# Cutting VectorE's routing of two heads into a key part and a pair part, in six gaps instead of three

## The chip, the cores and the metric

The kernel runs on one core of a Trainium2 chip. The metric is the device time of one execution in microseconds (us), the median of several runs. In the profile PE is TensorE's matmuls, PEld its weight loads, DVE VectorE, ACT ScalarE, POOL GpSimd and SP SyncE.

## The reference, cut to what matters

Two decoder layers over 256 tokens of width 1024. Layer 0 mixes tokens by a gated linear recurrence, layer 1 by dilated attention, and each is followed by a PEER expert layer. That one is where most of the time goes:

```python
q = (xn @ w_q).reshape(T, PEER_HEADS, PEER_DKEY)          # 8 heads
s1 = einsum('thd,nd->thn', q[..., :half], sub_keys[0])    # 128 keys each
s2 = einsum('thd,nd->thn', q[..., half:], sub_keys[1])
v1, i1 = lax.top_k(s1, 16);  v2, i2 = lax.top_k(s2, 16)
cand = (v1[..., :, None] + v2[..., None, :]).reshape(T, 8, 256)
cs, ci = lax.top_k(cand, 16)
experts = i1[ci // 16] * 128 + i2[ci % 16];  gates = softmax(cs)
act = gelu(xn . u[experts]) * gates
out = sum over the 128 experts of act * v[experts]
```

Each token gathers 128 rows of 4 KB from `u` and 128 from `v`.

## The kernel before

Tokens lie on the 128 partitions, in two tiles. Layer and tile make four phases: (0,0), (0,1), (1,0), (1,1). A phase's gather has 16 rounds, and a round handles eight experts of each token, half a head. GpSimd copies the eight indices to `idx_cur` and issues eight indirect DMAs into `u_ring` and eight into `v_ring` (eight slots each). An issue into a slot of u waits until VectorE has used the row before (L748, one instruction a row), one of v until TensorE has (L1240). VectorE multiplies each u row by the token and sums it, ScalarE takes a tanh (`ez`), VectorE writes the eight weights `act_w` (L762), ScalarE makes eight diagonal matrices `diag`, and TensorE adds diag times v row to `acc`, two matmuls of 512 columns a row.

All that a token tile needs before its gather (mixer, projection of the queries, key scores, routing) is written as generators with `yield`s, one set for each of the four compute engines, and `run` places their steps in the gaps between the rounds of the phase before: after round n, in gap n, each engine runs what `PLANS[phase][n]` names. "m" is the next step of the next phase's mixer and routing, "R" the next piece of this phase's own routing. Every engine works strictly in the order in which its program is written. In each gap VectorE's work comes behind `act_w` of that round and ahead of the u rows of the next. TensorE's comes behind the round's `acc` matmuls. ScalarE's comes behind the `diag`s and ahead of `ez` of the next round.

`PARTS` cuts the eight heads into (0), (1), (2, 3), (4, 5) and (6, 7). Heads 0 and 1 are routed with the steps of the phase before. Parts 2 to 4 are the "R" pieces, each in one gap: `route_part` on VectorE, one exponential of the gates on ScalarE, nothing on TensorE. GpSimd waits on `idx_ready` for the indices of a head, and head h is needed from round 2h.

The weights of mixers and projections come in 1 MB chunks on SP's queue into four slots of `w_ring`. SP issues the next chunk when TensorE has used the one four before.

Names for later: `tv`, `ti`, `tif` are the top 16 of a head's two key lists, `cand` their 256 sums, `cs`, `ci` the best 16 of these, `hot` (in the tile `xn`) a one-hot table that turns positions into key numbers. `xn` also holds the normed tokens that TensorE transposes for a mixer, hence the wait on `transposed` in `route_part`.

Of the kernel before, what the change touches and what calls it, by code (L numbers as in the profile page):

```python
# [35 lines left out]
TOPK = 16  # L36
PART = 2
PARTS = ((0, 1), (1, 1), (2, 2), (4, 2), (6, 2))
# [31 lines left out]


PLANS = {
    0: ["R", "m", "Rm", "R"] + ["m"] * 10 + ["", ""],
    1: ["R", "m", "Rm", "R"] + ["m"] * 11 + [""],
    2: ["R", "m", "Rm", "R"] + ["m"] * 11 + [""],
    3: ["R", "R", "R", ""],
}


class Chain:  # L80
# [10 lines left out]
    def link(self, ins):  # L91
        self.tick(ins)
        self.engine.wait_ge(self.sem, self.base + self.n if self.step is None else self.step + (self.base + self.n))
# [27 lines left out]
def build(nc, x_d, wall_d, gains_d, lb_d, headg_d, rope_d, amask_d, lmask_d, ident_d, iota_d, skt_d,  # L121
          u_d, v_d, out_d):
    ctx = ExitStack()
    with ctx:
# [3 lines left out]
        def sem(name):  # L128
            return ctx.enter_context(nc.semaphore(name))
# [63 lines left out]
        hot = xn[:, :].rearrange("p (m n) -> p m n", n=TOPK)  # L193
# [45 lines left out]
        transposed = sem("transposed")  # L239
# [17 lines left out]
        PHASE_OF = [(0, 0), (0, 1), (1, 0), (1, 1)]  # L257
# [119 lines left out]
        def _(dve):  # L377
# [3 lines left out]
            link, tick = chain.link, chain.tick  # L381
            count = Count()
# [4 lines left out]
            def wait_next(sem, n=1):  # L387
                dve.wait_ge(sem, count.next(sem.name, n))
# [17 lines left out]
            def token_rsqrt(t):  # L406

                link(V.scalar_tensor_tensor(out=xn[:, :], in0=h[:, t, :], scalar=1.0, in1=h[:, t, :],
                                            op0=ALU.mult, op1=ALU.mult, accum_out=ms[:, 0:1]))
                rsqrt(1, D)  # L410
# [6 lines left out]
            def scale_gain(t, gain, dst, scale):  # L417
                link(V.scalar_tensor_tensor(out=dst, in0=h[:, t, :], scalar=scale, in1=gains[:, gain, :],
                                            op0=ALU.mult, op1=ALU.mult))
                count.transposes += 1  # L420
                count.normed = count.transposes
                dve.sem_inc(to_transpose, 1)
# [216 lines left out]
                add_residual(t, 1, 1)  # L639
                dve.sem_inc(mixed, 1)  # L640

            def route_part(phase, p):

                layer, t = PHASE_OF[phase]
                lo, heads = PARTS[p]
                if p in (0, 2):

                    wait_next(projected)

                dve.wait_ge(transposed, count.normed)  # L650
                hot_n = hot[:, 0:2 * heads * TOPK, :]
                pairs = [(n, a) for n in range(heads) for a in range(2)]

                def each(ops, of):
                    for op in ops:
                        for m in of:
                            (link if op is ops[-1] and m is of[-1] else tick)(op(m))


                sc = lambda m: s_all[:, lo + m[0], m[1], :]  # L660
                first = lambda a, m: a[:, m[0], m[1], 0:8]
                last = lambda a, m: a[:, m[0], m[1], 8:16]
# [6 lines left out]
                for n in range(heads):  # L669
                    tick(tt(cand[:, n, :].rearrange("p (a b) -> p a b", a=TOPK), over(tv[:, n, 0, :], TOPK),  # L670
                            tv[:, n, 1:2, :].to_broadcast([P, TOPK, TOPK]), ALU.add))
                link(V.tensor_copy(tif[:, 0:heads, :, :], ti[:, 0:heads, :, :]))
                each([lambda n: V.max(cs[:, n, 0:8], cand[:, n, :])], range(heads))
                each([lambda n: V.max_index(ci[:, n, 0:8], cs[:, n, 0:8], cand[:, n, :]),
                      lambda n: V.match_replace(cand[:, n, :], cs[:, n, 0:8], cand[:, n, :], LOWEST)], range(heads))
# [30 lines left out]
            def route(phase):  # L706
                layer, t = PHASE_OF[phase]

                if phase == TILES:
                    dve.wait_ge(gain_in, 16)  # L710
                scale_gain(t, (GAIN_F0, GAIN_F1)[layer], xp[:, t, :], 1.0)
                token_rsqrt(t)
                link(V.tensor_copy(xr[:, t:t + 1], rs[:, 0:1]))
                dve.sem_inc(factor_ready, 1)
                yield

                dve.wait_ge(transposed, count.normed)
                link(V.tensor_scalar(xp[:, t, :], xp[:, t, :], xr[:, t:t + 1], None, ALU.mult))
                count.chunks += 8
                count.banks += 8  # L720
                route_part(phase, 0)
                yield
                route_part(phase, 1)
                yield rest(phase)

            def rest(phase):

                for p in range(2, len(PARTS)):
                    route_part(phase, p)
                    yield  # L730

            def mixer(phase):
# [66 lines left out]
            link(V.memset(ones[:, :], 1.0))  # L799
            dve.wait_ge(consts_in, 16 * EARLY)  # L800
            run(gather, mixer, route)


        @block.scalar
        def _(act):
            A = nc.scalar
            chain = Chain(act, act_side)
            link, tick = chain.link, chain.tick
            count = Count()
# [4 lines left out]
            def give(out, in_, func, **more):  # L814

                wait_next(argument)
                link(A.activation(out, in_, func, **more))  # L817
                act.sem_inc(value, 1)  # L818
# [111 lines left out]
            def route_part(phase, p):  # L930
                lo, heads = PARTS[p]
                g = gate_all[:, phase * SLOTS + lo * TOPK:phase * SLOTS + (lo + heads) * TOPK]
                give(g, g, ACT.Exp)

            def rest(phase):
                for p in range(2, len(PARTS)):
                    route_part(phase, p)
                    yield

# [65 lines left out]
        def _(pe):  # L1005
            M = nc.tensor.matmul
            count = Count()
# [169 lines left out]
            def rest(phase):  # L1177
                for p in range(2, len(PARTS)):
                    yield

            def route(phase):
                layer, t = PHASE_OF[phase]
                transpose_new([xp[:, t, n * P:(n + 1) * P] for n in range(KT_D)])
                turn_of = {}

                def queries(c):
                    project(1, True)
                    turn_of[c] = count.banks

                def scores(c):  # L1190
                    out = take_turn()

                    pe.wait_ge(bank_read, turn_of[c])
                    for b in range(4):
                        ins = M(out[:, b * P:(b + 1) * P], qpT[:, 4 * c + b, :], skt[:, layer, b % 2, :], start=True,  # L1195
                                stop=True)
                    ins.then_inc(scored, 1)

                queries(0)
                if phase == 0:  # L1200
                    pe.wait_ge(later_in, 16 * LATER)
                scores(0)
                yield
                queries(1)
                if phase == 0:

                    pe.wait_ge(w_used, WRING + count.chunks)
                    pe.sem_inc(u_used, RING)
                queries(2)
                scores(1)  # L1210
                scores(2)
                yield
                queries(3)
                if phase == 0:

                    pe.wait_ge(w_used, WRING + count.chunks)
                    pe.sem_inc(v_used, RING)
                scores(3)
                count.next(projected.name, 2)
                yield rest(phase)  # L1220
# [103 lines left out]
```

## Time and profile before

| | us |
|---|---|
| median of 3 runs | 1776.9 |
| lowest and highest | 1772.48 and 1778.13 |
| profiled execution, span from first to last instruction | 1768.2 |
| median less that span | 8.7 |
| TensorE busy | 1434.2 |
| VectorE busy | 1116.1 |
| GpSimd busy | 1143.6 |
| ScalarE busy | 276.3 |

The times of the runs are whole executions; the span is that of one profiled execution. Busy times are sums over the span, and an engine can be the one that sets the pace in one stretch and wait in the next.

### The profile page before, as it was taken

To read this page: it belongs to the slowest core of one execution; us is meant where nothing else is said; L and a number is where in the kernel's file an instruction comes from. 1 tells how busy PE (TensorE), PEld (TensorE's weight loads), DVE (VectorE), ACT (ScalarE), POOL (GpSimd) and SP (SyncE) were. 2 spreads that over 40 slices of the span, in tenths; PEclk is the share of its full clock that TensorE was granted. 3 is DMA by queue.
4 is the path that set the end of the run, shared out by engine and by line. 5 is a ranking of instruction groups with operands and counts; after the bars stand their busy time and mean duration, and the time that the engine had idled before them with its cause. 6 is when DMAs were issued, how large, how long until landed. Compare 5 with 4: busy or idle time off the path is not lost.

```text
span 1768.2 us, 18597 instructions
## 1 busy us (share of the span) xinstructions
PE 1434.2 (81%) x5144; PEld 835.4 (47%) x5144; DVE 1116.1 (63%) x2843; ACT 276.3 (16%) x757; POOL 1143.6 (65%) x1094
## 2 busy tenths in 40 slices
PE   7968797999898596988899778889789766776776
PEld 6867454655664253544357334454346422332332
DVE  2648786777463868475566578665567499444454
ACT  1211111211111111121111110122111101111111
POOL 0004777677657777767776676667775767777775
PEclk9989898999999898989899889899999987988889
DMA  8855999999999999999999999999999989999998
GB/s 321 307 217 178 352 414 410 410 411 410 413 399 411 341 370 392 377 381 384 374 413 412 386 322 413 358 408 374 372 397 411 339 317 326 354 358 369 368 389 327
DMA packets 164520, 649.13 MB, mean 367 GB/s; under 512 B 18656, under 2 KB 18912, under 8 KB 151648
## 3 DMA queue, kind: packets, MB, share of 16 engines
q0 software_dynamic: 147456, 536.94, 79.6%
q1 hardware_dynamic: 16992, 111.27, 15.8%
q8 instruction: 40, 0.66, 0.1%
q14 instruction: 32, 0.26, 0.0%
HBM read 647.09 MB, written 1.05 MB: 367 GB/s over the span
## 4 chain that ended last, share of the span: by engine, by line
PE 57%; DVE 21%; DMA 7%; issue 6%; POOL 5%; ACT 4%; POOLq 0%; DVEq 0%; ACTq 0%; SPq 0%; PEldq 0%
PE acc L1240 35%; PE bank L1061 9%; DVE u_ring L748 9%; PE bank L1057 8%; DMA u_ring<-in_u,idx_cur 6%; POOL v_ring L370 3%; POOL u_ring L370 2%; DVE xn L385 1%; ACT diag L988 1%; DVE arena L385 1%; ACT xT L825 1%; PE bank L1195 1%; DVE ef L692 1%; DMA v_ring<-in_v,idx_cur 1%; ACT arena L840 1%
## 5 line engine op out<-in xcount | busy, mean ns | idle before, releaser
L1240 PE MATMUL acc<-v_ring,diag 128*128 128x512 f32 x2040 | 972.8, 638 | 267.5 <-ACT diag L988 266.0
L1240 PEld LDWEIGHTS acc<-v_ring,diag 128*128 128x128 f32 x2040 | 413.2, 205 | 805.5 <-issue 569.1
L748 DVE SCALAR_TENSOR_TENSOR u_ring<-u_ring,xp 128x1024 f32<-128x1024 f32 x512 | 613.0, 1225 | 260.0 <-DMA u_ring<-in_u,idx_cur 250.0
L370 POOL DMA_INDIRECT v_ring<-in_v,idx_cur x512 | 578.5, 1130 | 270.4 <-PE acc L1240 135.5
L370 POOL DMA_INDIRECT u_ring<-in_u,idx_cur x512 | 539.7, 1054 | 195.0 <-issue 132.0
L1061 PE MATMUL bank<-w_ring,xT 128*128 128x256 f32 x768 | 171.9, 384 | 7.3 <-ACTq L826 7.3
L1061 PEld LDWEIGHTS bank<-w_ring,xT 128*128 128x128 f32 x768 | 146.6, 192 | 30.5 <-ACTq L826 8.9
L988 ACT ACTIVATE diag<-ident,act_w 128x128 f32<-128x128 f32 x510 | 156.2, 388 | 17.7 <-DVE act_w L762 15.9
L1057 PE MATMUL bank<-xT,w_ring 128*128 128x128 f32 x1280 | 148.4, 279 | 6.2 <-ACTq L826 6.2
L1057 PEld LDWEIGHTS bank<-xT,w_ring 128*128 128x128 f32 x1280 | 147.4, 195 | 11.4 <-ACTq L826 7.6
L762 DVE SCALAR_TENSOR_TENSOR act_w<-ez,gz 128x8 f32<-128x8 f32 x64 | 10.9, 170 | 197.1 <-ACT ez L983 197.1
L361 POOL COPY idx_cur<-idx_all 128x8 uint32 x64 | 23.4, 365 | 145.2 <-DVE idx_all L696 144.9
L983 ACT ACTIVATE ez<-zi 128x8 f32<-128x8 f32 x64 | 13.3, 208 | 539.9 <-DVEq L759 535.7
L840 ACT ACTIVATE arena<-bank 128x512 f32<-128x512 f32 (+1 forms) x54 | 30.3, 580 | 372.6 <-PE bank L1057 222.1
L385 DVE TENSOR_TENSOR arena<-arena 128x512 f32<-128x512 f32 (+3 forms) x57 | 42.9, 782 | 7.6 <-ACTq L818 4.4
L825 ACT ACTIVATE xT<-tr 128x512 f32<-128x512 f32 x26 | 14.2, 595 | 181.6 <-PE tr L1019 181.1
L748 DVE DVE_READ_ACCUMULATOR u_ring<-u_ring,xp 128x1 f32 x512 | 41.7, 81 | 0.0
L825 ACT ACTIVATE arena<-tr 128x512 f32<-128x512 f32 (+2 forms) x24 | 11.6, 524 | 152.8 <-PE tr L1173 106.8
L777 DVE COPY h<-acc 128x512 f32<-128x512 f32 x3 | 2.1, 692 | 47.1 <-PEq L1261 47.1
L817 ACT ACTIVATE arena<-arena 128x1024 f32<-128x1024 f32 x18 | 19.0, 1057 | 38.7 <-DVEq L425 38.4
L817 ACT ACTIVATE gate_all<-gate_all 128x32 f32<-128x32 f32 (+1 forms) x20 | 4.5, 224 | 124.0 <-DVEq L425 123.8
L385 DVE TENSOR_TENSOR h<-h,bank 128x512 f32<-128x512 f32 x8 | 5.5, 686 | 27.8 <-PE bank L1061 25.0
(128 smaller groups left out, 794.6 us busy)
## 6 DMA issues: line engine op xcount, KB each, us to landing
w_ring<-in_wall SPq DMA_DIRECT2D x92, 1024.0 KB, 8.5
u_ring<-in_u,idx_cur POOLq DMA_INDIRECT x512, 7.2
v_ring<-in_v,idx_cur POOLq DMA_INDIRECT x512, 7.1
u_ring<-in_wall SPq DMA_DIRECT2D x4, 1024.0 KB, 9.7
v_ring<-in_wall SPq DMA_DIRECT2D x4, 1024.0 KB, 9.8
gains<-in_gains SPq DMA_DIRECT2D x5, 512.0 KB, 13.4
h<-in_x SPq DMA_DIRECT2D x2, 512.0 KB, 9.1
arena<-in_amask SPq DMA_DIRECT2D x1, 576.0 KB, 10.3
```

Source lines behind the costliest of these rows:

```text
L361: nc.gpsimd.tensor_copy(idx_cur[:, g * RING:(g + 1) * RING], idx_all[:, bass.ds(i * TOPK + g * RING, RING)]).then_inc(idx_set, 1)
L370: nc.gpsimd.indirect_dma_start(out=ring[:, r, :], out_offset=None, in_=table, in_offset=bass.IndirectOffsetOnAxis(ap=idx_cur[:, g * RING + ...
L385: return V.tensor_tensor(out, a, b, op)
L692: link(V.tensor_reduce(ef[:, 0:heads, :, :].rearrange("p n a k -> p (n a k)"), hot_n, AX.X, ALU.add))
L748: V.scalar_tensor_tensor(out=u_ring[:, r, :], in0=u_ring[:, r, :], scalar=1.0, in1=xp[:, t, :], op0=ALU.mult, op1=ALU.mult, accum_out=z[:, ...
L817: link(A.activation(out, in_, func, **more))
L825: (link if n == len(copies) - 1 else tick)(A.activation(dst, src, ACT.Copy))
L840: A.activation(dst, source[:, first:first + width], func, scale=scale))
L988: A.activation(diag[:, r, :], ident[:, :], ACT.Copy, scale=act_w[:, g * RING + r:g * RING + r + 1]).then_inc(diag_ready, 1)
L1057: ins = M(out[:, (2 * c + b) * P:(2 * c + b + 1) * P], w[:, k, b * P:(b + 1) * P], xT[:, k, :], start=k == 0, stop=k == KT_D - 1)
L1061: ins = M(out[:, c * 256:(c + 1) * 256], xT[:, k, :], w[:, k, :], start=k == 0, stop=k == KT_D - 1)
L1240: ins = M(acc[:, s], diag[:, r, :], v_ring[:, r, s], start=False, stop=hi == ROUNDS and n == hi - lo - 1 and r == count_of - 1)
```

## The change

`route_part` of VectorE is cut in two. `key_part` finds the top 16 of the two key lists of each head, forms the 256 sums and casts the key numbers. `pair_part` finds the best 16 sums, the gates and the expert numbers, and gives `idx_ready`. For heads 0 and 1 both still run one after the other. For parts 2 to 4 there is a `yield` between them, so that there are six "R" pieces, and the plans are written anew. ScalarE and TensorE get empty pieces to match, and ScalarE's exponential goes with `pair_part`.

```diff
 PLANS = {
-    0: ["R", "m", "Rm", "R"] + ["m"] * 10 + ["", ""],
-    1: ["R", "m", "Rm", "R"] + ["m"] * 11 + [""],
-    2: ["R", "m", "Rm", "R"] + ["m"] * 11 + [""],
-    3: ["R", "R", "R", ""],
+    0: ["R", "Rm", "R", "Rm", "R", "Rm"] + ["m"] * 9 + [""],
+    1: ["R", "Rm", "R", "Rm", "Rm", "Rm"] + ["m"] * 9 + [""],
+    2: ["R", "Rm", "R", "Rm", "Rm", "Rm"] + ["m"] * 9 + [""],
+    3: ["R", "R", "R", "R", "R", "R"],
 }
...
-            def route_part(phase, p):
...
+            def key_part(p):
+
                 lo, heads = PARTS[p]
                 if p in (0, 2):
 
                     wait_next(projected)
-
-                dve.wait_ge(transposed, count.normed)
-                hot_n = hot[:, 0:2 * heads * TOPK, :]
                 pairs = [(n, a) for n in range(heads) for a in range(2)]
...
                 link(V.tensor_copy(tif[:, 0:heads, :, :], ti[:, 0:heads, :, :]))
+
+            def pair_part(phase, p):
+
+                layer, t = PHASE_OF[phase]
+                lo, heads = PARTS[p]
+                dve.wait_ge(transposed, count.normed)
+                hot_n = hot[:, 0:2 * heads * TOPK, :]
                 each([lambda n: V.max(cs[:, n, 0:8], cand[:, n, :])], range(heads))
...
-                route_part(phase, 0)
-                yield
-                route_part(phase, 1)
+                key_part(0)
+                pair_part(phase, 0)
+                yield
+                key_part(1)
+                pair_part(phase, 1)
                 yield rest(phase)
 
             def rest(phase):
 
                 for p in range(2, len(PARTS)):
-                    route_part(phase, p)
+                    key_part(p)
+                    yield
+                    pair_part(phase, p)
                     yield
...
 (ScalarE)
             def rest(phase):
                 for p in range(2, len(PARTS)):
+                    yield
                     route_part(phase, p)
                     yield
...
 (TensorE)
             def rest(phase):
                 for p in range(2, len(PARTS)):
                     yield
+                    yield
```

## Rows read from the trace of the kernel before

**Rows 1.** The page: span, engines, transfer rate by 40 slices, all transfers, issue to landing.
```profile
span 1768.2 us, 18597 instructions
...
PE 1434.2 (81%) x5144; PEld 835.4 (47%) x5144; DVE 1116.1 (63%) x2843; ACT 276.3 (16%) x757; POOL 1143.6 (65%) x1094
...
GB/s 321 307 217 178 352 414 410 410 411 410 413 399 411 341 370 392 377 381 384 374 413 412 386 322 413 358 408 374 372 397 411 339 317 326 354 358 369 368 389 327
DMA packets 164520, 649.13 MB, mean 367 GB/s; under 512 B 18656, under 2 KB 18912, under 8 KB 151648
...
u_ring<-in_u,idx_cur POOLq DMA_INDIRECT x512, 7.2
```

**Rows 2.** Windows by phase: us, busy us (PE to POOL), PEclk, DMA share, GB/s.
```profile
167.90:590.10 422.20, 366.47 (x1436) 222.38 (x1436) 286.54 (x714) 71.78 (x187) 298.92 (x282) 0.93 1.01 402
590.10:1001.20 411.10, 341.32 (x1118) 189.08 (x1118) 265.58 (x705) 63.23 (x188) 287.85 (x273) 0.92 0.99 384
1001.20:1411.30 410.10, 340.02 (x1154) 191.52 (x1154) 269.01 (x704) 66.26 (x192) 290.18 (x272) 0.95 0.99 377
1411.30:1753.80 342.50, 240.91 (x483) 102.28 (x484) 204.56 (x505) 42.56 (x144) 249.97 (x249) 0.85 0.96 358
```

**Rows 3.** Windows: phases 1 and 2, rounds 0-6; phase 3 rounds 2-4 and ten later ones, between issues.
```profile
590.10:778.90 188.80, 152.51 (x456) 85.91 (x456) 139.61 (x402) 27.64 (x83) 128.42 (x116) 0.92 0.97 373
1001.20:1190.60 189.40, 153.00 (x456) 86.15 (x456) 139.82 (x401) 27.67 (x83) 131.14 (x117) 0.92 0.98 372
1433.90:1509.80 75.90, 52.06 (x103) 22.34 (x104) 64.24 (x200) 11.29 (x38) 53.88 (x51) 0.80 0.92 327
1509.80:1734.20 224.40, 157.68 (x318) 66.71 (x317) 107.91 (x210) 26.53 (x90) 167.86 (x171) 0.86 0.98 371
```

**Rows 4.** Timeline of TensorE, phase 1; brackets: idle before and its releaser.
```profile
616.86 16.38 PE L1240 MATMUL acc<-v_ring,diag 128*128 128x512 f32 x32 [10.41 <-ACT diag L988]
...
635.33 7.17 PE L1061 MATMUL bank<-w_ring,xT 128*128 128x256 f32 x32 [1.22 <-ACTq L826]
644.15 14.00 PE L1240 MATMUL acc<-v_ring,diag 128*128 128x512 f32 x32 [1.65 <-ACT diag L988]
657.99 13.98 PE L1061 MATMUL bank<-w_ring,xT 128*128 128x256 f32 x64
...
700.07 15.73 PE L1240 MATMUL acc<-v_ring,diag 128*128 128x512 f32 x32 [12.38 <-ACT diag L988]
...
726.75 14.00 PE L1240 MATMUL acc<-v_ring,diag 128*128 128x512 f32 x32 [1.68 <-ACT diag L988]
```

**Rows 5.** Timeline of VectorE, phase 1, gap 0 and the start of gap 1.
```profile
590.02 0.87 DVE L663 MAX8 tv<-arena 128x8 f32<-128x128 f32 x4
...
596.17 0.75 DVE L673 MAX8 cs<-cand 128x8 f32<-128x256 f32 x2
...
605.93 1.22 DVE L748 SCALAR_TENSOR_TENSOR u_ring<-u_ring,xp 128x1024 f32<-128x1024 f32 x1
...
616.20 0.17 DVE L762 SCALAR_TENSOR_TENSOR act_w<-ez,gz 128x8 f32<-128x8 f32 x1 [0.33 <-ACT ez L983]
...
620.16 1.28 DVE L418 SCALAR_TENSOR_TENSOR xn<-h,hr,gains 128x1024 f32<-128x1024 f32 x1
```

**Rows 6.** Timeline of GpSimd: first and last of eight u issues, last v issue, round 1.
```profile
583.99 1.09 POOL L370 DMA_INDIRECT u_ring<-in_u,idx_cur  x1 [0.83 <-POOL idx_cur L361]
...
593.87 0.94 POOL L370 DMA_INDIRECT u_ring<-in_u,idx_cur  x1 [0.30 <-issue]
...
607.26 1.85 POOL L370 DMA_INDIRECT v_ring<-in_v,idx_cur  x1 [0.78 <-PE acc L1240]
```

**Rows 7.** Windows of single rounds of phase 1: gaps 0, 3 and 5.
```profile
590.10:616.40 26.30, 15.86 (x32) 6.75 (x32) 25.05 (x86) 2.88 (x10) 17.79 (x17) 0.82 0.89 320
...
673.20:699.60 26.40, 14.00 (x32) 6.00 (x32) 25.15 (x85) 2.89 (x10) 16.33 (x15) 0.82 1.02 408
...
726.30:756.80 30.50, 28.47 (x102) 18.87 (x102) 17.19 (x45) 4.72 (x13) 19.73 (x19) 1.00 1.02 410
```

More of the change, by code:

```diff
@@ L640, in attention, with each @@
                 dve.sem_inc(mixed, 1)
-            def route_part(phase, p):
-                layer, t = PHASE_OF[phase]
+            def each(ops, of):
+                for op in ops:
+                    for m in of:
+                        (link if op is ops[-1] and m is of[-1] else tick)(op(m))
+            def key_part(p):
                 lo, heads = PARTS[p]
@@ L648, in route_part @@
                     wait_next(projected)
-                dve.wait_ge(transposed, count.normed)
-                hot_n = hot[:, 0:2 * heads * TOPK, :]
                 pairs = [(n, a) for n in range(heads) for a in range(2)]
[L654 to L657, printed above, removed]
                 sc = lambda m: s_all[:, lo + m[0], m[1], :]
```

## The prediction

> **What bounds the kernel now.** I read the page first. TensorE is busy 81% of the span and VectorE 63% [rows 1]. Neither is full, so I went on to the line of GB/s: it stands at 410 to 414 in many of the 40 slices and never above [rows 1]. I take 410 GB/s as what this program's transfers reach when enough of them are in flight.
>
> Next the windows by phase [rows 2]. Each phase has 16 rounds and moves 134 MB of gathered rows (16 rounds of 16 rows of 4 KB for 128 tokens), and phases 0 to 2 also stream weights for the next phase. Phase 0 runs at 402 GB/s, phase 1 at 384, phase 2 at 377, phase 3 at 358. So phase 0 is already near what the queues deliver, and the later ones are not. What is lost in phases 1 and 2 can be narrowed: the first seven rounds of phase 1 take 188.8 us at 373 GB/s [rows 3], which is 70.4 MB. At 410 they would take 171.8 us. At most 17.0 us lie there, and the same in phase 2, whose first seven rounds take as long to within a microsecond [rows 3].
>
> Then the order of time on TensorE in those rounds [rows 4]. A round of `acc` takes 14.0 us straight after other work and 15.7 to 16.4 us after a wait. After it comes the step of the next mixer, if the gap has one: gap 1 has transposes and a projection (633.2 to 642.5), gap 2 a projection of 13.98. Between such work TensorE waits only some 1.7 us for the weights of the next round. But it waits 10.41 us before the round at 616.86 (so round 0 had ended at 606.45) and 12.38 us before the one at 700.07. These follow gaps 0 and 3, the two in which VectorE routes and no mixer step runs.
>
> VectorE's timeline says why [rows 5]. After `act_w` of round 0 it routes two heads from 590.02 to 605.93, multiplies eight rows of u, and has `act_w` at 616.20. That is 15.9 + 10.3 = 26.2 us, longer than TensorE's 16 or so, and also longer than the 22.4 us per round of ten later rounds of phase 3, which have nothing in their gaps [rows 3]. In gaps 0 and 3 the routing of two heads sets the pace. In gap 2 it does not, since `acc` and projection together take longer.
>
> **The change part by part.** *Cut.* The key part K runs from the first MAX8 on the scores up to the first MAX8 on the candidates: 590.02 to 596.17, so 6.1 us. The pair part P is 596.17 to 605.93, 9.8 us [rows 5]. No VectorE, ScalarE or TensorE instruction is added. Only the wait for the transposes goes from the head of K to the head of P, and there it is satisfied: the transposes are TensorE work of an earlier gap, done before TensorE's next round, while P stands behind VectorE's next round. In phase 3 rounds 4 and 5 are written out instead of looped, which I price at nothing.
>
> *Placed.* K has gaps 0, 2, 4 and P gaps 1, 3, 5. In phases 1 and 2 mixer steps stand in gaps 1, 3, 4, 5 and on, instead of 1, 2, 4, 5. One step alone, the second, moves. In phase 0 every step from the second is a gap later, and the last is in gap 14 instead of 13. The indices of heads 2 and 3 come one gap later, and round 4 is the first to need them, so GpSimd does not wait. A step that moves takes its weight transfers along, since SP issues each chunk when TensorE has used the one four before.
>
> *Phase 1 walked through.* I use 10.3 us from the first row of u to `act_w`, 0.7 us to the first matmul, 1.0 us from the end of a projection to `act_w` [rows 4, 5], and a median of 7.2 us from issue to landing [rows 1]. Eight issues on GpSimd take 9 to 10 us (583.99 to 593.87 [rows 6]).
> Gap 0 holds K: VectorE is free at 596, but the last row of u for round 1 is issued at 593.87 [rows 6] and lands near 601. `act_w` comes at 603.5, and `acc` can start only when the round before has ended, at 606.5. Before, it started at 616.86: 10 us gained.
> Gap 1 holds P and step 1. VectorE needs 9.8 and 5.3 us (616.20 to 621.44 [rows 5]), so TensorE's transposes can start 15.1 us after `act_w`, at 618.6, while its `acc` runs to 623. Hidden. The step ends at 632.2, `act_w` at 633.2 against 643.5.
> Gap 2 holds K alone. VectorE could have `act_w` at 633.2 + 6.1 + 10.3 = 649.6. The rows of u set it: GpSimd starts their issue about 2 us after the last v row of round 2. The u rows of round 2 start at 609.5 (before at 610: the v rows of round 1 wait for `acc` of round 0, to 607.26 [rows 6]), eight u and eight v issues take 20, so this is about 631.5. Eight issues take 9 to 10 more, landing under load some 10 by my estimate (7.2 the median), so 652.5 against 673.0 (0.2 before the window that begins at 673.20 [rows 7]).
> Gap 3 holds P and step 2: 0.7 + 15.7 + 14.0 + 1.0 = 31.4 on TensorE gives 684 against 699.4. VectorE's 20.1 is hidden.
> Gap 4 has K and step 3, gap 5 P and step 4. TensorE's own sums there, 25 and 30.5 us, hold `act_w` at 709 and 740, against 726.1 and 756.6. VectorE was busy 17.19 us of the 30.5 of gap 5 [rows 7] and has 9.8 more, 27.0, still under. So the engines alone allow 16 us.
> This is as much as the bytes allow (17.0). Two limits that meet are not both reached: rows that land late hold VectorE, and 4 MB of weights after step 2 fall into the next two rounds. I take 12 us. Bounds are 17 and, if only the transfers' idle time of round 0 is won (a share of 0.89 against 1.02 where they are full, over 26.3 us [rows 7]), 3.4, say 4. Phase 2 repeats phase 1: 12 us again. Afterwards the phase runs on as before, shifted.
>
> *The ceiling by a page.* The slices have up to 414 GB/s [rows 1]. The Trainium skill ("DMA: Bandwidth & Descriptors", Where 436 GB/s comes from) says that from HBM to SBUF the memory side binds at about 358 GB/s per core, though its own single-core table has 425. By the first figure all transfers would be at their limit already, at 367 over the whole span, and the change would be worth nothing. By that rule the trace disagrees.
>
> *Phase 3.* Three gaps of routing. From the first issue of round 2 to that of round 5 pass 75.9 us at 327 GB/s, and the next ten rounds take 224.4, or 22.4 each [rows 3]. With K (6.1 + 10.3) or P (9.8 + 10.3) in a gap VectorE needs at most 20.1. Three rounds then take 67.3 us, 8.6 less. The start of the stretch hangs on v rows that wait for `acc` of round 0 and doesn't move. I take 8, bounds 4 and 10.
>
> *Phase 0.* At 402 of 410 GB/s there are 8 us at most in 422. The loss is in rounds 0 and 1, and part of it is v rows that wait for TensorE. The step in gap 14 makes that round longer, which the earlier rounds give in advance. I take 2, bounds −3 and 5.
>
> *Sum.* 2 + 12 + 12 + 8 = 34 us. The profiled execution has a span of 1768.2 [rows 1], the median of the runs is 1776.9, and I leave the 8.7 around it as it is: span 1734, median 1743.
>
> **Rivals.** *The queues take most of it back.* Weights of steps 2 and 4 and the gathers compete, the earlier issue only lengthens landing, and K-only rounds come out at 26 us as before. For it: in gap 5 the queues already stand at 1.02 and 410 GB/s [rows 7]. Against it: 327 and 373 GB/s in [rows 3]. Price: 4 + 4 in phases 1 and 2, 4 in phase 3, 0 in phase 0, so 12: 1765.
>
> *The change does nothing for the time.* The 649 MB go at the mean 367 GB/s of the span [rows 1] whatever VectorE does: a round that is issued earlier lands no earlier, because the memory delivers no more. Then 649.13 / 0.367 is the span of now, and the time 1777. Against it are the 414 in [rows 1]; for it, that the ten later rounds of phase 3 average only 371 [rows 3]. The page's rule, named above, is this case.
>
> *Slower: P stands in front of the mixer step and makes TensorE wait.* In gap 1 P and step 1 need 15.1 us, and the start of `acc` and its matmuls cover 14.7 to 17.1 [rows 4]. Every microsecond over goes into the round. There are nine gaps with P and a step. It decides when the lateness reaches 34 / 9 = 3.8 us in each. With 5 us in each, 45 − 34 = 11 more: 1788. Against it is that in walking no gap came out over 0.5.
>
> **How the numbers follow.** The forecast has 0.64, the queues 0.18, nothing 0.09, slower 0.09. Forecast's own range: gains 14 to 48, or 1729 to 1763. The range for 8 in 10 goes from 1730 to 1768, and takes in the rival of the queues; what is left out is mostly nothing and slower. 0.3% is 5.3 us, about what a measurement of this kernel can tell from no change. Faster 0.82, same 0.09, slower 0.09.
>
> **What would show it.** Right: TensorE's waits of 10.4 and 12.4 us before round 1 and round 4 of phase 1 go below 2, and a new one of some 5 us stands before round 3; the first seven rounds take 174 to 180 us at over 390 GB/s; phase 3's stretch from round 2 to 5 takes 67 to 69 us; phase 0 stays within 5 us of 422.2. Wrong: K-only rounds still take 26 us, with VectorE waiting for `u_ring` transfers (the queues); TensorE's transposes in gap 1 wait for VectorE (slower); phase 0 grows by more than 5 us because gap 14's step is not repaid.

## The result and the profile after

| | us |
|---|---|
| before, median of 4 runs | 1777.52 (1772.48 to 1779.26) |
| after, median of 4 runs | 1724.84 (1722.64 to 1728.74) |
| ratio after / before | 0.9724, 95% interval 0.9695 to 0.9753 |
| span of the profiled execution, before and after | 1768.2 and 1723.6 |
| time of the profiled execution after | 1725.8 |

The kernel is 52.7 us faster, where 34 were forecast, and the time lies 5 us below the range. From profile to profile the span is 44.6 us shorter. Ratios here and below are worked out from undisturbed (fast) runs alone and medians from all runs, so on the slower chips a table's two times do not divide to its ratio exactly.

The page of the changed kernel, lines that answer to [rows 1]:

```profile
span 1723.6 us, 18557 instructions
...
PE 1422.7 (83%) x5144; PEld 830.7 (48%) x5144; DVE 1118.4 (65%) x2843; ACT 276.1 (16%) x757; POOL 1135.0 (66%) x1094
...
GB/s 325 301 241 147 379 397 411 412 412 411 405 412 411 363 367 405 411 411 410 394 406 412 411 364 412 411 412 408 394 402 410 328 330 372 373 371 367 372 378 308
DMA packets 164522, 649.15 MB, mean 377 GB/s; under 512 B 18656, under 2 KB 18912, under 8 KB 151648
...
u_ring<-in_u,idx_cur POOLq DMA_INDIRECT x512, 9.5
```

VectorE executes the same 2843 instructions. The transfer rate has more slices at 405 to 412, and the median from issue to landing of a row of u rose from 7.2 to 9.5 us: rows are issued earlier and then wait longer to be delivered.

Windows by phase, as [rows 2], and below them the stretches of [rows 3] (rounds 0 to 6 of phases 1 and 2, phase 3 from the issue of round 2 to that of round 5, and ten later rounds):

```profile
167.80:588.00 420.20, 366.32 (x1436) 222.42 (x1436) 286.11 (x714) 71.80 (x188) 300.23 (x283) 0.94 1.02 404
588.00:980.60 392.60, 334.73 (x1118) 186.50 (x1118) 267.41 (x704) 63.17 (x189) 282.99 (x273) 0.95 1.01 398
980.60:1373.70 393.10, 335.93 (x1154) 189.74 (x1154) 269.54 (x704) 66.22 (x192) 283.57 (x273) 0.96 1.01 396
1373.70:1709.30 335.60, 240.34 (x483) 102.03 (x484) 204.88 (x504) 42.35 (x144) 251.49 (x250) 0.86 0.98 365
```

```profile
588.00:764.10 176.10, 149.84 (x456) 84.79 (x456) 140.79 (x401) 27.66 (x83) 129.48 (x118) 0.95 1.00 389
980.60:1156.50 175.90, 150.29 (x456) 84.96 (x456) 140.51 (x401) 27.63 (x83) 126.79 (x118) 0.95 1.01 400
1396.00:1463.10 67.10, 45.42 (x90) 19.26 (x89) 54.52 (x162) 8.19 (x28) 50.87 (x52) 0.83 0.98 365
1463.10:1688.70 225.60, 158.49 (x321) 67.31 (x320) 118.36 (x246) 26.76 (x91) 169.20 (x170) 0.86 0.99 373
```

By phase the gains between these two profiles are 2.0, 18.5, 17.0 and 6.9 us, against 2, 12, 12 and 8 forecast. Of the 18.5 in phase 1, 12.7 come in rounds 0 to 6 (188.8 to 176.1), and of the 17.0 in phase 2 13.5 (189.4 to 175.9). That is about what was forecast for each whole phase. TensorE's timeline of these rounds, as [rows 4]:

```profile
588.43 30.59 PE L1247 MATMUL acc<-v_ring,diag 128*128 128x512 f32 x64 [8.92 <-ACT diag L994]
619.46 1.09 PE L1025 MATMUL tr<-ident,xn 128*128 128x128 f32 x8 [0.44 <-DVEq L422]
621.77 7.17 PE L1067 MATMUL bank<-w_ring,xT 128*128 128x256 f32 x32 [1.22 <-ACTq L831]
...
655.11 15.95 PE L1247 MATMUL acc<-v_ring,diag 128*128 128x512 f32 x32 [9.56 <-ACT diag L994]
670.89 13.98 PE L1067 MATMUL bank<-w_ring,xT 128*128 128x256 f32 x64
686.59 14.00 PE L1247 MATMUL acc<-v_ring,diag 128*128 128x512 f32 x32 [1.72 <-ACT diag L994]
```

The 64 matmuls in the first line are rounds 0 and 1 with no wait between them. That is where 10.41 us stood. The 12.38 us before round 4 are 1.72. A new wait of 9.56 us stands before round 3, where K has the gap alone. The transposes of gap 1 wait 0.44 us for VectorE, so P in front of the mixer step comes out just at the edge of its cover. Phase 2 has the same wait, 0.46 us, and the other seven gaps with P and a step have none.

VectorE's timeline shows the cut as it was costed, as [rows 5] (the second row is the last piece of K, then `act_w` of round 1, P's first and the mixer step's first instruction):

```profile
587.85 0.87 DVE L657 MAX8 tv<-arena 128x8 f32<-128x128 f32 x4
...
593.74 0.24 DVE L666 CAST tif<-ti 128x64 f32<-128x64 uint32 x1
594.01 1.22 DVE L753 SCALAR_TENSOR_TENSOR u_ring<-u_ring,xp 128x1024 f32<-128x1024 f32 x1
...
604.28 0.17 DVE L767 SCALAR_TENSOR_TENSOR act_w<-ez,gz 128x8 f32<-128x8 f32 x1 [0.33 <-ACT ez L989]
604.36 0.74 DVE L674 MAX8 cs<-cand 128x8 f32<-128x256 f32 x2
...
614.14 1.30 DVE L408 SCALAR_TENSOR_TENSOR xn<-h 128x1024 f32<-128x1024 f32 x1
```

K takes 6.2 us and P 9.8. The windows of gaps 2, 4 and 5 of phase 1 (the last answers to the row of gap 5 in [rows 7]):

```profile
630.20:654.70 24.50, 14.24 (x32) 5.92 (x32) 16.45 (x57) 2.68 (x10) 18.53 (x20) 0.88 1.02 404
...
686.20:711.20 25.00, 22.05 (x72) 12.93 (x72) 17.83 (x58) 4.42 (x13) 17.57 (x17) 1.00 1.03 414
711.20:741.70 30.50, 28.47 (x102) 18.88 (x102) 26.23 (x73) 4.93 (x15) 20.88 (x19) 1.00 1.02 412
```

In gap 2 VectorE is busy only 16.45 of 24.5 us, and the transfers run at 404 GB/s: this round waits for rows of u. In gaps 3 to 5 TensorE's own matmuls set the pace, with 31.5, 25.0 and 30.5 us a round, as the walk had it.

### The profile page after: what moved, and what is told of

Its sections match the earlier page's. It is cut to its first block, busy times and chain, and to the rows that moved or that the text cites. A ratio compares the mean times of both kernels' runs of the same rounds, so it can differ in the third digit from the quotient of the medians.

```text
span 1723.6 us, 18557 instructions
## 1 busy us (share of the span) xinstructions
PE 1422.7 (83%) x5144; PEld 830.7 (48%) x5144; DVE 1118.4 (65%) x2843; ACT 276.1 (16%) x757; POOL 1135.0 (66%) x1094
## 4 chain that ended last, share of the span: by engine, by line
PE 57%; DMA 13%; issue 9%; POOL 9%; DVE 8%; ACT 4%; POOLq 0%; DVEq 0%; SPq 0%; ACTq 0%; PEldq 0%
PE acc L1247 36%; DMA u_ring<-in_u,idx_cur 10%; PE bank L1063 9%; PE bank L1067 8%; POOL v_ring L370 5%; DVE u_ring L753 4%; POOL u_ring L370 3%; DMA v_ring<-in_v,idx_cur 2%; ACT diag L994 1%; PE bank L1202 1%; DVE arena L385 1%; ACT xT L830 1%; ACT arena L845 1%; PE tr L1025 1%; PE scp L1081 1%
## 5 line engine op out<-in xcount | busy, mean ns | idle before, releaser
L1247 PE MATMUL acc<-v_ring,diag 128*128 128x512 f32 x2040 | 960.7, 632 | 233.7 <-ACT diag L994 230.3
L1247 PEld LDWEIGHTS acc<-v_ring,diag 128*128 128x128 f32 x2040 | 408.6, 203 | 764.3 <-issue 556.4
L370 POOL DMA_INDIRECT u_ring<-in_u,idx_cur x512 | 532.7, 1041 | 198.3 <-issue 128.2
L1067 PEld LDWEIGHTS bank<-w_ring,xT 128*128 128x128 f32 x768 | 146.6, 192 | 30.5 <-ACTq L831 8.9
L822 ACT ACTIVATE arena<-arena 128x1024 f32<-128x1024 f32 x18 | 19.0, 1057 | 44.8 <-DVEq L425 44.6
L1202 PE MATMUL bank<-skt,arena 128*128 128x128 f32 x128 | 17.5, 282 | 6.6 <-ACTq L846 6.6
```

The source lines that it names most:

```text
L370: nc.gpsimd.indirect_dma_start(out=ring[:, r, :], out_offset=None, in_=table, in_offset=bass.IndirectOffsetOnAxis(ap=idx_cur[:, g * RING + ...
L1067: ins = M(out[:, c * 256:(c + 1) * 256], xT[:, k, :], w[:, k, :], start=k == 0, stop=k == KT_D - 1)
L1247: ins = M(acc[:, s], diag[:, r, :], v_ring[:, r, s], start=False, stop=hi == ROUNDS and n == hi - lo - 1 and r == count_of - 1)
```

## The experiments

Kernels of one session ran on one chip, beside runs of the kernel before, and ratios are within a session. The sessions differ: in the second and third (A, B below) before took 1768 us, in the first, fourth and fifth 1917, 1890 and 1890, with transfers slower and more uneven for every kernel. Each session had another chip and no chip had two, so the runs can't tell the chip from the occasion; "fast chip" and "slow chip" below mean these sessions. I read sizes from the two faster chips and quote the others for completeness.

### What lies around the span

The kernel before, unchanged, on the chip where everything takes 8% longer.

> The kernel before, timed and profiled once more, to see what lies between a run's span and its time. Theory A (the profiled execution of before was a short one): each run's time is its span plus some 2 us, as it is after the change (1725.8 against 1723.6), and ordinary spans are 1774 to 1777, not 1768.2. Theory B (something outside the span takes 8.7 us in this kernel): spans of 1767 to 1770 with times of 1777.

1918.9 us, ratio 1.0042 (1.0007 to 1.0077) to itself: a hint that intervals of this chip are too narrow by some 0.4%. All ten runs have 1.8 us between span and time (the profiled one 1907.2 and 1909.0). The changed kernel has 2.2. Theory B is out. By theory A the profiled execution of before, with its span of 1768.2, took about 1770 (an estimate, its own time is not on record), less than each of its four timed runs. The spans of 1774 to 1777 that the theory expects of ordinary runs could not be checked on this chip. On session A's chip ordinary runs of before took 1761 to 1778.

### The phases one by one

The new plan in some phases and the old places, written with both parts in one gap, in the others. For phases 1 and 2 alone:

```diff
-    0: ["R", "Rm", "R", "Rm", "R", "Rm"] + ["m"] * 9 + [""],
+    0: ["RR", "m", "RRm", "RR"] + ["m"] * 10 + ["", ""],
     1: ["R", "Rm", "R", "Rm", "Rm", "Rm"] + ["m"] * 9 + [""],
     2: ["R", "Rm", "R", "Rm", "Rm", "Rm"] + ["m"] * 9 + [""],
-    3: ["R", "R", "R", "R", "R", "R"],
+    3: ["RR", "RR", "RR", ""],
```

> The new plan in phases 1 and 2 alone, phases 0 and 3 as before. Theory A (rows of u and v that are issued earlier than they can land pile up and are delivered in rounds 7 to 11 at over 400 GB/s): 35 to 40 us faster than before, and in phase 1 rounds 7 to 10 take 20.4 us each with 8 to 12 us from issue to landing. Rival (the gain in rounds 7 to 15 was chance of TensorE's clock): 24 to 28 us, and rounds 7 to 10 take 21.5 to 22 us as before.

> The new plan in phase 3 alone. If the phases add up: 7 us faster, 4 to 10. Rival (phase 3's profit needs the earlier phases' lead): under 3 us.

> The new plan in phase 0 alone, with its last step in gap 14. If the queues are full there already: within 4 us of before. Rival (the profile of before hid a larger loss in phase 0, as its ordinary runs are longer): 6 us or more faster.

The first two fell on the slow chip: 0.9866 (0.9813 to 0.992), which is 26 us and in the rival's range, and 0.999 (0.9952 to 1.0028). So I ran them again, with the changed kernel:

> The changed kernel once more, on whichever chip this is. Theory A (the working of the span is right within some 10 us, and 8 us of the measured 52.7 came from a profile of before that was shorter than its runs): 40 to 48 us faster than before where before takes 1765 to 1770, phases 1 and 2 at 391 to 394 us each. Rival (the change is worth 50 us and more everywhere): 50 to 56.

> The new plan in phases 1 and 2 alone, again, since the first chip it ran on takes 8% longer for every kernel. Theory A: 30 to 36 us faster, rounds 0 to 6 of phase 1 at 176 us and rounds 7 to 11 at 102 to 104. Rival: 24 to 28, rounds 7 to 11 at 105 to 107.

> The new plan in phase 3 alone, again. If the phases add up: 5 to 10 us faster, the stretch from the issue of round 2 to that of round 5 at 67 to 70 us instead of 76. Rival: under 3.

| kernel | us | before | ratio, 95% interval |
|---|---|---|---|
| all phases (session B) | 1726.62 | 1768.21 | 0.9755, 0.9715 to 0.9796 |
| phases 1 and 2 (B) | 1738.28 | 1768.21 | 0.9822, 0.9786 to 0.9858 |
| phase 3 (B) | 1761.83 | 1768.21 | 0.9961, 0.9936 to 0.9986 |
| phase 0 (session A) | 1767.56 | 1767.78 | 1.0003, 0.9982 to 1.0024 |

In medians 41.6, 29.9, 6.4 and 0.2 us. The phases add up to 36.5 of 41.6, inside the intervals. For phases 1 and 2 the 29.9 us lie at the lower edge of what theory A expected (30 to 36) and above the rival's 24 to 28. Phase 0 gives nothing that can be measured, at 402 GB/s with the old plan and 404 with the new one. The profile of phases 1 and 2 alone, then that of phase 0 alone (whose phases 1 and 2 have the old plan), phase 1 of the changed kernel run again, and phase 3's stretch from the issue of round 2 to that of round 5 in the kernel with phase 3 alone:

```profile
586.80:980.10 393.30, 332.30 (x1118) 185.59 (x1118) 265.97 (x704) 63.14 (x189) 285.90 (x275) 0.95 1.01 403
980.10:1373.30 393.20, 338.17 (x1154) 191.02 (x1154) 268.84 (x704) 66.30 (x192) 283.22 (x273) 0.96 1.00 394
```

```profile
165.80:585.60 419.80, 365.76 (x1436) 222.16 (x1436) 286.57 (x715) 71.89 (x188) 297.35 (x283) 0.94 1.02 404
585.60:991.10 405.50, 335.56 (x1118) 186.53 (x1118) 266.56 (x705) 63.27 (x189) 284.71 (x273) 0.94 0.99 386
991.10:1397.30 406.20, 340.49 (x1154) 191.69 (x1154) 268.78 (x705) 66.32 (x193) 290.10 (x273) 0.95 0.99 383
```

```profile
588.30:984.40 396.10, 337.45 (x1118) 187.74 (x1118) 266.61 (x704) 63.12 (x188) 282.23 (x273) 0.94 1.01 398
```

```profile
1428.40:1499.70 71.30, 44.70 (x89) 18.87 (x88) 54.45 (x162) 8.20 (x28) 55.05 (x51) 0.82 0.95 344
```

One execution of a phase is not like another, so here are phases 1 and 2 of every profile on the faster chips, cut in three: us in rounds 0 to 6, 7 to 11 and 12 to 15.

| profile | plan | phase 1 | phase 2 |
|---|---|---|---|
| before | old | 188.8, 106.7, 115.6 | 189.4, 105.4, 115.3 |
| phase 0 alone | old | 189.3, 103.0, 113.1 | 188.2, 105.8, 112.2 |
| phase 3 alone | old | 188.6, 102.1, 115.1 | 188.7, 109.0, 116.6 |
| after | new | 176.1, 104.0, 112.5 | 175.9, 102.0, 115.3 |
| after, again | new | 176.8, 103.5, 115.8 | 175.0, 102.3, 115.7 |
| phases 1 and 2 alone | new | 176.4, 102.8, 114.1 | 174.9, 101.9, 116.4 |
| step stays (next section) | new | 175.9, 102.6, 113.2 | 176.8, 102.9, 113.0 |

With the new plan phase 1 takes 391.7 to 396.1 us (391 to 394 were expected) and phase 2 392.7 to 393.2, with the old one 405.4 to 411.1 and 406.2 to 414.3. Means are 14 and 17 us apart. Most of that stands in rounds 0 to 6, 12.6 and 13.1 us, and every profile has it. Rounds 7 to 11 of phase 2 are 4.5 us shorter in the mean, and no new profile reaches an old one. In phase 1 the difference there is 0.7 us, less than profiles of one plan lie apart.

Phase 3 up to the last issue of a v row takes 342.5, 349.8 and 347.6 us with the old plan (before, phase 0 alone, phases 1 and 2 alone) and 335.6, 338.8, 341.4 and 340.9 with the new one (after, after again, phase 3 alone, step stays). Its stretch from round 2 to 5 took 71.3 us in the kernel with phase 3 alone, above the 67 to 70 expected, against 67.1 in the first profile after and 75.9 before.

### The step's place, and the places without the cut

In phases 1 and 2 the second mixer step stays in gap 2 (phase 2's line, changed alike, is left out here):

```diff
-    1: ["R", "Rm", "R", "Rm", "Rm", "Rm"] + ["m"] * 9 + [""],
+    1: ["R", "Rm", "Rm", "R", "Rm", "Rm"] + ["m"] * 9 + [""],
```

> As the changed kernel, but in phases 1 and 2 the second mixer step stays in gap 2 behind K, so that gap 3 holds P alone. If moving the step matters: P alone needs 9.8 + 10.3 us and K with the step 31 us, the sum of the two gaps stays what it was, so within 3 us of the changed kernel. Rival (weights that come a gap later or earlier change how full the queues are): 5 us or more apart, slower.

1731.21 us, ratio 0.9802 (0.9776 to 0.9828) (session A). Phase 1 takes 391.7 us and its rounds 0 to 6 176.0, phase 2 392.7, the same as after the change. In these two phases it makes no difference that can be seen where the second step stands. The whole is 36.6 us faster than before, 5.0 less than the changed kernel in the other session. The intervals overlap, and phase 3, whose plan is the same, is 5.3 us longer here than in the first profile after, so a small loss is neither shown nor ruled out.

```profile
588.20:979.90 391.70, 333.08 (x1118) 185.94 (x1118) 267.68 (x704) 63.13 (x188) 279.27 (x273) 0.95 1.01 400
979.90:1372.60 392.70, 337.59 (x1154) 190.49 (x1154) 270.25 (x705) 66.28 (x193) 281.16 (x273) 0.96 1.01 396
588.20:764.20 176.00, 150.09 (x456) 84.80 (x456) 141.07 (x401) 27.65 (x83) 126.07 (x118) 0.95 1.00 395
```

The reverse has the new places and no cut: both parts in gaps 0, 2 and 4, nothing in 1, 3, 5 but the steps (phases 0 and 2, changed alike, are left out here).

```diff
-    1: ["R", "Rm", "R", "Rm", "Rm", "Rm"] + ["m"] * 9 + [""],
-    3: ["R", "R", "R", "R", "R", "R"],
+    1: ["RR", "m", "RR", "m", "RRm", "m"] + ["m"] * 9 + [""],
+    3: ["RR", "", "RR", "", "RR", ""],
```

> The mixer steps stand where the change puts them, but both parts of the routing of two heads run together in gaps 0, 2 and 4 (phase 3 too). If the cut gives the gain: VectorE needs 26 us a round in three gaps instead of two without a step, so no faster than before, 0 to 15 us slower. If the new places give it: over half of the gain, 25 us or more faster.

> Steps in the new places, both parts together in gaps 0, 2 and 4, again. If the cut gives the gain: within 10 us of before, on either side. If the places give it: 20 us or more faster.

1.0052 (1.0015 to 1.0089) on the slow chip, and in session B 1784.3 us, 1.0083 (1.0049 to 1.0118): 16 us slower than before. That is more than the 10 I had allowed. In phases 0 to 2 the new places without the cut give no gain, they lose, so there the cut is what gives it. Windows of phases 0 and 1, of rounds 0 to 6 of phase 1, and of phase 3 from the issue of round 2 to that of round 5:

```profile
167.30:597.50 430.20, 363.14 (x1436) 221.16 (x1436) 285.94 (x714) 71.82 (x187) 301.99 (x283) 0.93 1.01 395
597.50:1016.80 419.30, 346.35 (x1118) 191.42 (x1118) 265.93 (x704) 63.25 (x188) 291.28 (x273) 0.91 0.98 377
597.50:792.20 194.70, 156.60 (x456) 88.05 (x456) 139.79 (x401) 27.66 (x83) 130.26 (x117) 0.89 0.95 360
1457.50:1525.00 67.50, 48.85 (x102) 21.12 (x103) 52.94 (x163) 10.84 (x37) 51.26 (x52) 0.85 0.97 362
```

Against the profile of before phases 0 and 1 lose 8 us each and phase 2 loses 7. Phase 3 does not: 67.5 us for its three rounds, as with the cut (67.1), and 336.5 us for the phase up to the last v row. Where there are no mixer steps, whole pieces with an empty gap behind each give the same as the cut, so in phase 3 it is the new places that gain. The cut is needed where steps fill the gaps.

### What paces the rounds that have room

GpSimd copies 16 indices a head instead of 8 a round (shown is the copy; `idx_cur` is doubled and the loop goes over two heads):

```diff
-                    nc.gpsimd.tensor_copy(idx_cur[:, g * RING:(g + 1) * RING],
-                                          idx_all[:, bass.ds(i * TOPK + g * RING, RING)]).then_inc(idx_set, 1)
+                    nc.gpsimd.tensor_copy(idx_cur[:, j * TOPK:(j + 1) * TOPK],
+                                          idx_all[:, bass.ds(i * (2 * TOPK) + j * TOPK, TOPK)]).then_inc(idx_set, 1)
```

> As the changed kernel, but GpSimd copies the 16 indices of a head at once instead of 8 for each round, so that every second round has no copy and no wait for it. Theory A (rounds without a backlog, all of phase 3, are paced by GpSimd's issues): the ten later rounds of phase 3 take 21.7 to 22.1 us instead of 22.4, the whole 6 to 12 us less than the changed kernel, with phase 0 unchanged. Rival (the queues pace phase 3, at 371 GB/s): no change, within 2 us.

> The kernel before with the same copy of 16 indices at once. Theory A: phase 3 and rounds 7 to 11 of phases 1 and 2 gain 0.6 us each, 8 to 15 us in all. Rival (queues pace them): nothing.

1711.83 us, ratio 0.9696 (0.9671 to 0.9721), and in the kernel before 1753.55, 0.9917 (0.9888 to 0.9946). The profile of the changed kernel with it, and below it phases 1, 2 and the ten later rounds of phase 3 of the kernel before with it:

```profile
167.40:584.60 417.20, 364.22 (x1436) 221.65 (x1436) 287.49 (x715) 71.84 (x188) 290.37 (x275) 0.95 1.02 407
584.60:976.60 392.00, 334.14 (x1118) 186.05 (x1118) 266.55 (x704) 63.11 (x188) 277.40 (x264) 0.95 1.01 401
976.60:1369.40 392.80, 338.10 (x1154) 191.16 (x1154) 269.87 (x704) 66.27 (x192) 276.28 (x265) 0.96 1.00 394
1457.00:1674.20 217.20, 164.00 (x324) 68.98 (x323) 120.28 (x258) 26.78 (x92) 163.45 (x165) 0.86 1.00 387
```

```profile
589.40:996.60 407.20, 337.15 (x1118) 187.68 (x1118) 265.84 (x704) 63.28 (x189) 282.00 (x264) 0.93 0.99 385
996.60:1403.60 407.00, 341.86 (x1154) 192.52 (x1154) 268.89 (x704) 66.31 (x193) 283.87 (x265) 0.94 0.99 381
1501.90:1718.60 216.70, 159.45 (x320) 67.38 (x319) 107.83 (x210) 26.53 (x90) 162.89 (x166) 0.86 1.00 388
```

The ten later rounds of phase 3 take 217.2 us instead of 225.6, so 21.7 a round, at 387 GB/s instead of 373, and 216.7 in the kernel before. With 8 indices at a time they take 224 to 230 in every profile on a fast chip. They are paced by GpSimd's issue. Phase 0, expected unchanged, takes 417.2 us, where the seven profiles of the old and the new plan with 8 at a time have 418.9 to 422.2. The whole is 14.8 us below the changed kernel of the other session, more than the 6 to 12 expected.

Phases 1 and 2 stay at 392.0 and 392.8: after the change a cheaper issue wins nothing there. It doesn't show before the change either, with 407.2 and 407.0 among old phases of 405.4 to 414.3, so these totals don't tell the two theories apart. Rounds 7 to 11 of phase 2 do, faintly: with the cheaper issue 103.2 us in the kernel before, under its three other values (105.4 to 109.0), and 102.0 in the changed one, among the 101.9 to 102.9 it has anyway. In phase 1 they are 104.4 and 103.1, within the spread. Nor are transfers the limit through the whole phase. From 868 to 970 us, which are rounds 12 to 15 of phase 1 after the change, `acc` (55%) and the projections (28%) fill the chain of work that ended last, with no transfer in it.

The opposite, a needless second copy and wait in each round, was to show whether rounds 7 to 11 are covered by a backlog:

```diff
+                    for again in range(2):
+                        if again:
+                            pool.sem_inc(pool_tick, 1)
                         nc.gpsimd.tensor_copy(idx_cur[:, g * RING:(g + 1) * RING], ...
+                        pool.wait_ge(idx_set, i * (2 * GROUPS) + (2 * g + again + 1))
```

> The changed kernel with a needless second copy of the eight indices and its wait, some 1.2 us of GpSimd a round. Theory A (backlog): where rows land 8 us and more after their issue, the queues stay full and nothing is lost, in phases 1 and 2 from round 3 on and in phase 0; phase 3, with 6 us to landing, loses 1.2 us a round, 16 to 20 in all; rounds 7 to 11 of phases 1 and 2 lose 0 to 3 us a phase. Rival (the issue paces rounds 7 to 11 after the change too): 6 us for each of the two.

> The kernel before with the same second copy. Theory A: phase 3 loses 1.2 us a round where VectorE doesn't pace it, about 14, and rounds 7 to 11 of phases 1 and 2, where no backlog stood before, lose 4 to 6 us a phase, more than after the change. Rival (the same everywhere): equal losses in rounds 7 to 11 before and after the change.

> The changed kernel with one copy of 16 indices a head, again, beside the changed kernel on the same chip: 8 to 16 us faster than it, nearly all in phase 3, and the fastest of all kernels of this study.

> The changed kernel, to stand beside the three others of this call on the same chip: 38 to 50 us faster than before.

> The changed kernel with the needless second copy, again, since the chip of the call before took 6% longer for every kernel. Theory A (backlog): on a chip with before at about 1770, phase 0 and rounds 0 to 6 of phases 1 and 2 unchanged, rounds 7 to 11 at 103 to 106 us (102 to 104 without the copy), phase 3's ten later rounds 10 to 12 us longer. Rival: rounds 7 to 11 at 108 to 110.

> The kernel before with the second copy, again. Theory A: rounds 7 to 11 of phases 1 and 2 at 109 to 112 us (103 to 107 without the copy), so a larger loss than after the change; phase 3's ten later rounds 10 to 12 us longer. Rival: the same loss in rounds 7 to 11 as after the change.

| kernel | us | before | ratio, 95% interval |
|---|---|---|---|
| after | 1848.69 | 1890.25 | 0.9846, 0.9784 to 0.9909 |
| after, copied twice | 1844.5 | 1890.25 | 0.9808, 0.9752 to 0.9863 |
| after, 16 at once | 1863.72 | 1890.25 | 0.9887, 0.982 to 0.9954 |
| before, copied twice | 1894.07 | 1890.25 | 1.0025, 0.9976 to 1.0074 |
| after, copied twice (last session) | 1838.55 | 1889.57 | 0.9715, 0.9666 to 0.9765 |
| before, copied twice (last session) | 1891.15 | 1889.57 | 0.9977, 0.9938 to 1.0016 |

Both sessions met slow chips. There 200 us of the middle of phase 0 in the changed kernel run at 373 GB/s with a DMA share of 0.98, where the profile above has 410 and 1.02:

```profile
300.00:500.00 200.00, 181.65 (x652) 111.13 (x651) 134.78 (x267) 40.11 (x95) 140.39 (x130) 0.94 0.98 373
```

Nothing is decided by these pairs: on such a chip the second copy doesn't show in the median at all (1844.5 against 1848.69, 1894.07 and 1891.15 against 1890). Their profiles don't settle it either: rounds 7 to 11 of phase 1 take 111.9 us with the second copy and 117.5 without it on the same chip, so chance outweighs what was looked for. Nor is the copy of 16 a gain there: its median is 15 us above the changed kernel's, with intervals that overlap. So it is the fastest kernel on a fast chip (session A), though not shown beside the changed kernel on one, and no gain on a slow one.

## Why the prediction was right and where it was wrong

**Bound and mechanism: right.** VectorE's routing paced the rounds after gaps 0 and 3. The waits of TensorE there went from 10.41 and 12.38 us to none and 1.72. Without the cut the new places are slower than before (1.0083). Of the signs named, rounds 0 to 6 came at 176.1 and 175.9 us (174 to 180), at 389 and 400 GB/s (over 390).

**The walk through phase 1: right in its sum.** It put `act_w` of rounds 5 and 6 at 119.1 and 150.1 us after that of round 0; the windows have 123 and 154 (from 588.0 to 711.2 and 741.7). Gap 0 took 16.6 us where it had 13.6: VectorE was free only at 594.0, and the eight rows of u take it 10.3 us from there up to `act_w`. The walk had VectorE free at 596 and `act_w` at 603.5, which leaves 7.5 us for work that it prices at 10.3. Gap 1 made this up, with 25.6 instead of 29.7. Gap 2, with K alone, took 24.5 instead of 19.3, since the rows of u for round 3 were issued later than worked out: 45.2 us after the start of the first window, where the walk had 41.4. The last of them landed some 10 us after its issue, as estimated.

```profile
633.17 0.96 POOL L370 DMA_INDIRECT u_ring<-in_u,idx_cur  x1 [0.83 <-POOL idx_cur L361]
```

The wait before round 3, given as some 5 us, is 9.56. Rounds 0 to 6 together gained 12.7 us in phase 1 and 13.5 in phase 2, where 12 were forecast, so "I take 12 us" held for the rounds it was worked out for.

**Phases 1 and 2: a term was put at nothing.** The step that failed is "Afterwards the phase runs on as before, shifted". The phases gained 18.5 and 17.0 us between the two profiles, and 14 and 17 in the means of all profiles on fast chips, so 29.9 to 35.5 for the two where 24 were forecast. Behind round 6 the two profiles have 5.8 and 3.5 us. Rounds 7 to 11, first phase 1 before and after, then phase 2:

```profile
778.90:885.60 106.70, 91.88 (x230) 42.93 (x231) 59.21 (x122) 18.32 (x58) 80.74 (x83) 0.91 0.99 373
```

```profile
764.10:868.10 104.00, 91.05 (x230) 42.57 (x231) 59.18 (x122) 18.26 (x59) 78.05 (x81) 0.91 1.02 401
```

```profile
1190.60:1296.00 105.40, 91.48 (x267) 46.06 (x268) 62.58 (x122) 21.35 (x63) 80.36 (x80) 0.97 0.99 371
```

```profile
1156.40:1258.40 102.00, 90.45 (x267) 45.53 (x268) 62.49 (x123) 21.36 (x62) 76.92 (x80) 0.98 1.02 399
```

They went from 373 to 401 and from 371 to 399 GB/s. Only phase 2's gain holds in the other profiles. In phase 1 two profiles with the old plan have 103.0 and 102.1 us, no more than the new ones, so its 2.7 us are not shown to be the change's. The queue's own view of the four rounds of phase 1 from the issue of round 8 says what changed, before first, then after:

```profile
DMA packets 9158, 33.37 MB, mean 371 GB/s; under 512 B 1016, under 2 KB 1016, under 8 KB 9155
...
u_ring<-in_u,idx_cur POOLq DMA_INDIRECT x33, 6.2
```

```profile
DMA packets 9818, 35.77 MB, mean 406 GB/s; under 512 B 1091, under 2 KB 1091, under 8 KB 9816
...
u_ring<-in_u,idx_cur POOLq DMA_INDIRECT x33, 8.6
```

A row lands 8.6 us after its issue instead of 6.2, and in phase 2 8.4 instead of 6.1. My reading: rows that were issued early in the crowded rounds 2 to 6 wait in the queues, and are delivered in rounds that used to be paced by GpSimd. What the two meeting limits kept back in the first seven rounds comes out behind them. It rests on these views, on the 4.5 us of phase 2 and on its rounds 7 to 11 answering to a cheaper issue before the change alone. The experiment meant to show it by itself was lost to slow chips, so the cause is argued, not shown. The rest of phase 1's difference, some 3 us, lies in rounds 12 to 15 and goes with TensorE's granted clock, whatever the plan: 115.6 us at 0.95 before and 112.5 at 0.98 after, but also 113.1 at 0.98 with the old plan (phase 0 alone) and 115.8 at 0.95 with the new one (after, again).

**Phases 3 and 0: right in size.** The stretch of three rounds went from 75.9 to 67.1 us (forecast 67.3), though one other profile of the new plan has 71.3. The phase gained 6.9 between the two profiles, 7.4 in the means of all and 6.4 in its own experiment (forecast 8). There the placing would have done it without the cut. Phase 0 gave 2.0 in the profile and 0.2 in its own experiment (forecast 2), so nothing that stands out from the spread.

**The sum: its last step failed.** "I leave the 8.7 around it as it is": the span is 1.8 to 2.2 us short of the time in every run where both are recorded. The profiled execution of before was itself, by the estimate of 1770.0, 7.5 us faster than the median. 44.2 us between the profiled executions (1770.0 to 1725.8), 7.5 for this and 1.0 for the one after (above its median) make the 52.7. In session B, with before at 1768, the same kernels are 41.6 apart. So of the missing 19 us 11.5 are phases 1 and 2 (less 1 in phase 3), as these two profiles have them, and some 8 are the base, which is a matter of runs. A gain of 41.6 is inside the forecast's 14 to 48; 52.7 is above even the 49 that the upper bounds of the four phases add up to. The lower bounds add up to 9, not to the 14 of the text.

**The rivals.** The queues did not take the gain back. The transfers were not at their limit before: the mean over the span is 377 GB/s now against 367. P in front of a mixer step made TensorE wait 0.44 us in gap 1 of phase 1, so that rival's place was right, and the wait was a tenth of the 3.8 us that it needed in each of nine gaps. The Trainium skill ("DMA: Bandwidth & Descriptors", Where 436 GB/s comes from) has the memory side bind at about 358 GB/s, and its table for one core alone goes to 425. This one-core program does not keep to 358: its profile shows 398 GB/s over the whole of phase 1.

## What to carry to other kernels

Long pieces of side work on the engine that frees a ring's slots cost where the piece and the engine's own round exceed the pace of the others; cut them at a point where nothing is handed on, and lay the parts into different rounds. Where gaps are empty, spreading whole pieces does the same. When the transfers have a ceiling in one stretch and lie below it in the next, work issued earlier need not be lost when the ceiling is met: count bytes over the whole phase and not over the stretch that was changed (here argued, from 4.5 us in one phase). Take the base of a sum from the same execution's time, not from a median. And before explaining a few microseconds between two profiles, look whether other executions of the same plan repeat them: phase 1 of one plan differed by up to 6 us.

## What the runs showed that I had not expected

One kernel takes 1768 us on two chips and 1890 to 1917 on three others. The slower ones move the same 649 MB. In the middle of phase 0, where the profile of before on a faster chip has 399 to 414 GB/s in every slice, its profile on the slowest has 309 to 397. The changed kernel itself ran on one of the slower chips only, with 0.9846 (0.9784 to 0.9909) against 0.9755 on a faster one, and a cheaper issue on GpSimd gave nothing there.
